# Two routers of a two-layer backbone get expert groups beside them, taken from the stages behind

## The reference

```python
def peer(h, wq, keys, u_tab, v_tab):
    q = (x @ wq).reshape(N, PEER_HEADS, 2, PEER_DKEY // 2)          # 8 heads
    s = jnp.einsum('nhpd,hpkd->nhpk', q, keys)                      # 2 x 128 scores
    top_s, top_i = lax.top_k(s, K)                                  # K = 16, twice
    cand = top_s[:, :, 0, :, None] + top_s[:, :, 1, None, :]
    best_s, best = lax.top_k(cand.reshape(N, PEER_HEADS, K * K), K)
    ...
    expert = (i1 * PEER_NKEYS + i2).reshape(N, PEER_HEADS * K)      # 128 experts a token
    gate = jax.nn.softmax(best_s, axis=-1)
    ...
        a = jax.nn.gelu(jnp.einsum('tkd,td->tk', u_tab[eb], xb), approximate=False)
        return jnp.einsum('tk,tkd->td', gb * a, v_tab[eb])
```

## Time and profile before

| what | us |
|---|---|
| median of 3 runs | 5934.2 |
| lowest and highest | 5932.68, 5950.15 |
| the profiled execution | 5949.2 |
| its span, first to last instruction | 5947.1 |
| PE busy in it | 4117.5 (69%) |
| DVE busy | 2900.9 (49%) |
| ACT busy | 1697.3 (29%) |
| POOL busy | 1441.5 (24%) |
| gathers, as a share of the 16 DMA engines | 56.4% |
| loads by SP, as such a share | 16.6% |
| mean granted TensorE clock | 0.814 |

### The profile page before, as it was taken

One profiled execution on the slowest core, in us unless ns is written; L12 is line 12 of the kernel. 1 busy time (PEld: TensorE's weight loads), 2 busy tenths in 40 slices (PEclk: granted clock), 3 DMA queues, 4 the chain that ended last, 5 costly groups with the idle time before them and its releaser, 6 DMA issues.

```text
span 5947.1 us, 63889 instructions
## 1 busy us (share of the span) xinstructions
PE 4117.5 (69%) x22248; PEld 2506.1 (42%) x22248; DVE 2900.9 (49%) x6835; ACT 1697.3 (29%) x4733; POOL 1441.5 (24%) x1295
## 2 busy tenths in 40 slices
PE   3889477889886685548476677778468785545555
PEld 1677454566563443224132235677335453211111
DVE  0321747544438544664445444322854445654444
ACT  0200137332432342233322222201152442222222
POOL 0000022212221232223343341000023332235443
PEclk7779789969997897778788888669778898767777
DMA  6434367748886798679999995024378997689998
GB/s 257 151 130 162 121 248 281 290 170 319 329 343 234 302 420 328 266 274 386 379 409 411 394 420 200 27 67 155 117 286 361 369 402 318 256 335 421 407 417 358
DMA packets 259315, 1712.65 MB, mean 288 GB/s; under 512 B 37712, under 2 KB 39344, under 8 KB 71600
## 3 DMA queue, kind: packets, MB, share of 16 engines
q0 software_dynamic: 184320, 1342.26, 56.4%
q1 hardware_dynamic: 74672, 366.31, 16.6%
HBM read 1690.43 MB, written 17.92 MB: 287 GB/s over the span
## 4 chain that ended last, share of the span: by engine, by line
PE 42%; DMA 24%; DVE 15%; ACT 6%; issue 4%; DVEq 4%; POOL 3%; ACTq 2%; SPq 1%; PEldq 0%; PEld 0%; POOLq 0%
PE psum L423 25%; DMA arena<-in_uv,arena 21%; PE psum L774 10%; DVE arena L2020 3%; POOL arena L1108 3%; DVE arena L1932 1%; DVE arena L1925 1%; DMA arena<-in_w_ada 1%; DVE arena L1926 1%; PE psum L383 1%; PE psum L604 1%; PE psum L605 1%; ACT arena L1444 1%; ACT arena L1441 1%; PE psum L639 1%
## 5 line engine op out<-in xcount | busy, mean ns | idle before, releaser
L1108 POOL DMA_INDIRECT arena<-in_uv,arena x1280 | 1437.6, 1123 | 4469.9 <-PE psum L774 3039.1
L774 PE MATMUL psum<-arena 64*64 64x512 f32 x10240 | 1564.5, 742 | 1086.5 <-ACTq L1445 990.9
L2020 DVE CUSTOM_DVE_ANT_0 arena<-arena 128x1024 f32<-128x1024 f32 x1280 | 1552.5, 1226 | 1330.0 <-DMA arena<-in_uv,arena 1272.4
L423 PE MATMUL psum<-arena 128*128 128x256 f32 (+2 forms) x8480 | 1945.9, 388 | 171.4 <-DVEq L1464 120.4
L423 PEld LDWEIGHTS psum<-arena 128*128 128x128 f32 (+1 forms) x8480 | 1616.9, 195 | 599.2 <-issue 194.1
L774 PEld LDWEIGHTS psum<-arena 64*64 64x64 f32 x10240 | 392.7, 157 | 2068.6 <-ACTq L1445 1375.8
L1438 ACT ACTIVATE arena<-arena 128x2 f32<-128x2 f32 x640 | 130.9, 205 | 1684.8 <-DVEq L2022 1671.3
L1444 ACT ACTIVATE arena<-arena 128x64 f32<-128x64 f32 x1280 | 376.2, 340 | 45.8 <-issue 1.8
L383 PE MATMUL psum<-arena 128*128 128x128 f32 (+1 forms) x680 | 129.4, 346 | 337.3 <-DVE arena L1523 119.8
L1441 ACT ACTIVATE arena<-arena 128x1 f32<-128x1 f32 x1280 | 307.6, 287 | 45.5 <-issue 1.3
L383 PEld LDWEIGHTS psum<-arena 128*128 128x128 f32 (+1 forms) x680 | 97.9, 178 | 391.2 <-issue 183.5
(11 more groups left out here) (210 smaller groups left out, 2747.4 us busy)
## 6 DMA issues: line engine op xcount, KB each, us to landing
arena<-in_w_in SPq DMA_DIRECT2D x92, 1024.0 KB, 5.9
arena<-in_w_mix SPq DMA_DIRECT2D x120, 768.0 KB, 7.3
arena<-in_w_ada SPq DMA_DIRECT2D x32, 1536.0 KB, 16.4
arena<-in_w_wq SPq DMA_DIRECT2D x40, 1152.0 KB, 6.0
arena<-in_w_wo SPq DMA_DIRECT2D x20, 1024.0 KB, 7.5
arena<-in_uv,arena POOLq DMA_INDIRECT x1280, 10.8
arena<-ada_rows SPq DMA_DIRECT2D x15, 512.0 KB, 5.6
arena<-x_rows SPq DMA_DIRECT2D x14, 512.0 KB, 6.2
```

Of the source, the lines that this page charges most:

```text
L423: ins = mm(out, a, b, start=(i == 0), stop=(i == last))
L774: ins = mm(psum[o, r_ * 512:r_ * 512 + 512], DIAG[rows, c, :], RING[rows, sl, D + half * 512:D + (half + 1) * 512], start=first, stop=last ...
L1108: pool.indirect_dma_start(RING[:, sl, :], None, io["uv"], bass.IndirectOffsetOnAxis(IDX[:, t, h * TOPK + k:h * TOPK + k + 1], 0)).then_inc ...
L2020: V_.tensor_tensor_reduce(out=RING[:, sl, 0:D], in0=RING[:, sl, 0:D], in1=XT[:, u % 2, :], scale=1.0, scalar=0.0, op0=ALU.mult, op1=ALU.ad ...
```

## The change

route(0,0) moves from the end of segment a to the start of b, and route(1,1) from the end of d to the start of e1, so that the groups of b and e1 are also spread over them. The order of the dense work stays as it was. The cost of a step of these two routers is 28 instead of 12, which only weighs how many groups they get. Since the groups beside these routers are of the tiles that the router is routing, `quotas` has a cap: behind step n of a router, no group of head n or later of its own pair may stand (`routed_upto`).

```diff
@@ steps
     if kind == "route":
-        return [12.0] * PH
+        return [(28.0 if (l, pairs) in FIRST_ROUTES else 12.0)] * PH
+FIRST_ROUTES = ((0, (0,)), (1, (1,)))
@@ schedule
-    a = [(k, 0, (0,)) for k in ("norm1", "qkv", "da", "mlp", "ml", "mc", "mln", "merge", "route")]
-    b = [(k, 0, both) for k in ("norm1", "qkv", "da", "mlp", "ml", "mc", "mln")] + [("merge", 0, (1,)), ("route", 0, (1,))]
+    a = [(k, 0, (0,)) for k in ("norm1", "qkv", "da", "mlp", "ml", "mc", "mln", "merge")]
+    b = [("route", 0, (0,))] + [(k, 0, both) for k in ("norm1", "qkv", "da", "mlp", "ml", "mc", "mln")] + [("merge", 0, (1,)), ("route", 0, (1,))]
-    d = [..., ("mln", 1, (1,)), ("merge", 1, (1,)), ("route", 1, (1,))]
-    e1 = [("q", 1, (2,)), ("da", 1, (2,)), ...]
+    d = [..., ("mln", 1, (1,)), ("merge", 1, (1,))]
+    e1 = [("route", 1, (1,)), ("q", 1, (2,)), ("da", 1, (2,)), ...]
+def routed_upto(items, l, pairs, heads):
+    for i, item in enumerate(items):
+        if item is not None:
+            (ul, t), g = UNITS[item[0]], item[1]
+            if (ul, (t // 2,)) == (l, pairs) and g * GS // TOPK >= heads:
+                return i
+    return len(items)
@@ quotas
-            for cost in steps(*st):
+            for n, cost in enumerate(steps(*st)):
                 cum += cost
                 want = lead + int(round((len(items) - lead) * cum / total))
+                if st[0] == "route" and n < PH - 1:
+                    want = max(done, min(want, routed_upto(items, st[1], st[2], n)))
```

More of the change, by code:

```diff
@@ L118, in schedule @@
     both = (1, 2)
-    a = [(k, 0, (0,)) for k in ("norm1", "qkv", "da", "mlp", "ml", "mc", "mln", "merge", "route")]
-    b = [(k, 0, both) for k in ("norm1", "qkv", "da", "mlp", "ml", "mc", "mln")] + [("merge", 0, (1,)), ("route", 0, (1,))]
+    a = [(k, 0, (0,)) for k in ("norm1", "qkv", "da", "mlp", "ml", "mc", "mln", "merge")]
+    b = [("route", 0, (0,))] + [(k, 0, both) for k in ("norm1", "qkv", "da", "mlp", "ml", "mc", "mln")] + [("merge", 0, (1,)), ("route", 0, (1,))]
     c1 = [("merge", 0, (2,)), ("route", 0, (2,))] + [(k, 1, (0,)) for k in ("norm1", "kv", "mlp", "ml")]
     c2 = [(k, 1, (1,)) for k in ("norm1", "qkv", "mlp", "mc")]
-    d = [("norm1", 1, (2,)), ("kv", 1, (2,)), ("mlp", 1, (2,)), ("edge", 1, (2,)), ("da", 1, (1,)), ("ml_back", 1, both), ("mln", 1, (1,)), ("merge", 1, (1,)), ("route", 1, (1,))]
-    e1 = [("q", 1, (2,)), ("da", 1, (2,)), ("ml_on", 1, both), ("mc", 1, (2,)), ("mln", 1, (2,)), ("merge", 1, (2,)), ("route", 1, (2,))]
+    d = [("norm1", 1, (2,)), ("kv", 1, (2,)), ("mlp", 1, (2,)), ("edge", 1, (2,)), ("da", 1, (1,)), ("ml_back", 1, both), ("mln", 1, (1,)), ("merge", 1, (1,))]
+    e1 = [("route", 1, (1,)), ("q", 1, (2,)), ("da", 1, (2,)), ("ml_on", 1, both), ("mc", 1, (2,)), ("mln", 1, (2,)), ("merge", 1, (2,)), ("route", 1, (2,))]
     p0 = sequence([0, 1])
```

## The result

| | us |
|---|---|
| before, median of 5 runs (the 3 of above and 2 more) | 5940.6 (5932.7 to 5950.2) |
| changed kernel, median of 5 runs | 5973.2 (5962.3 to 5992.1) |
| ratio, with its 95% interval | 1.0054 (1.004 to 1.0067) |
| forecast, range | 5959, 5910 to 6000 |
| the profiled execution of the changed kernel, its span | 5992.1, 5989.9 |

The kernel became slower by 32.6 us, 0.54%. The forecast was 24.8 us slower than the median it started from.

The account below looks back on a forecast made before the run. Lone routers were taken as VectorE chains with idle transfers, the first layer as bound by PE, the last stretch by transfers. 123 + 196 - 47 - 18 - 229 = +25 us on the median 5934.2 gave 5959, range 5910 to 6000.

Parts of the forecast that it names:

- Router (0,0), +123: Router (0,0), from 0 to 30 groups: 278.6 us against 155.7, so 123 us longer.
- Router (1,1), +196: Router (1,1), from 0 to 45 groups: 352.3 us against 156.1, so 196 us longer.
- the rival in which bursts are no dearer: Router (1,1) pays 4.07 us a group, as router (1,2) does, 183 us: +12, 5946 us, no change; chance 0.27.
- The value for each group past the fifth: In router bursts, each group past the fifth costs 5.2 us, the transfer rate.
- The rest of the first stretch, -47: Dense stages of segment b lose 26 groups at 1.88 us each and da(0,(1,2)) three: 47 us less.
- Router (0,1), -18: Router (0,1) has fewer groups; its first period falls from 32.9 to 22.6 us, three others by 2.6: 18 us less.
- The rest of the last stretch, -229: 45 groups leave merge(1,2), mc, da, ml_on, q and router (1,2): 229 us less, or 5.1 us a group.
- the two limits of 243 and 245: Merge(1,2) with 33 groups: PE's work takes 243 us, transfers at 402 GB/s take 245; forecast 249.
- What was charged nothing: Segments c1, c2, d and the tail keep their quotas, so no time was added for them.
- The last stretch gives more: All 45 groups leaving the last stretch give 6.1 us each, 275 in place of 229: 5913 us; chance 0.16.
- The slow rival, 243: Every group of router (1,1) pays 5.4 us, 243 in place of 196: +72, 6006 us; chance 0.13.

Follow-up runs that it names:

- the run with 8 groups: Only router (0,0) moved, its head cost 6 in place of 28, so 8 groups in place of 30, against the kernel before: 5942.1 us, ratio 0.9996.
- 17, 24 and 45 groups: Only router (1,1) moved, with head cost 8, 12 or 28, against the kernel before: ratios 0.9987, 1.0027 and 0.9947.

## Why the prediction was right, point by point

- **Router (0,0), +123.** +125.4. Its burst of seven took 50.0 us where I had 49.3, and the fours 34.6 to 35.0.
- **Router (1,1), +196.** +194.2, well above the 183 of the rival in which bursts are no dearer, and far from 243. The value for each group past the fifth, the transfer rate, is what the trace shows: 5.0 us a group. In the first burst of eight the fifth group ended 20.7 us behind the mark where I had 20.3, and three more at 5.0 us made 35.6 where I had 35.9. The periods of eight then came out 0.3 to 0.7 us shorter than said, that of seven 1.3 longer.
- **The rest of the first stretch, -47.** -39. Most dense stages gave what was said (mlp -14, ml -8, mc -10, merge(0,1) -11), but norm1 behind router (0,0) grew from 34.2 to 43.9 us. This is a cost that the record did not have: I followed SP's queue past XT and XP and charged nothing, but did not look at the loads behind the router. The token rows of norm1:

```profile
879.49 1.60 POOL L1121 DMA_INDIRECT arena<-in_uv,arena  x1 [0.31 <-issue]
...
880.45 1.25 SPq L901 DMA_DIRECT2D arena<-in_x  x2
893.08 1.06 ACT L1160 ACTIVATE arena<-arena 128x1024 f32<-128x1024 f32 x1 [16.11 <-DMA arena<-in_x]
```

  In the changed kernel they are issued behind gathers that POOL has just started (six in the 11 us before, of which the last is shown), and ScalarE has them 12.6 us later. In the kernel before nothing was under way, and it took 5.1 us:

```profile
751.98 0.80 SPq L888 DMA_DIRECT2D arena<-in_x  x2
...
757.06 1.06 ACT L1147 ACTIVATE arena<-arena 128x1024 f32<-128x1024 f32 x1 [10.29 <-DMA arena<-in_x]
```

  With one group a head (the run with 8 groups) POOL has issued nothing for 32 us when the load is issued; it takes 4.9 us again and norm1 36.4. So 7.5 of the 9.7 us are the late landing, and 2.2 stay without it. That the gathers delay the load is so supported from both sides; a run that issues the load earlier was not made.

  The shortfall of 8 us from the -47 can't be put to norm1 alone, though. In the run with the first move alone the same stages hold the same groups and norm1 is as long (43.4), and yet they fell by 48.8. The difference is ml(0,(1,2)); here it is in the kernel before (14 groups), in the changed kernel and in that run (11 each):

```profile
1191.10:1352.40 161.30, 136.20 (x728) 94.57 (x728) 82.35 (x202) 48.27 (x116) 30.00 (x26) 0.68 0.48 184
1310.90:1464.70 153.80, 133.41 (x680) 98.77 (x680) 72.81 (x188) 44.46 (x101) 23.82 (x23) 0.66 0.42 151
1309.70:1455.20 145.50, 124.84 (x680) 91.28 (x680) 72.83 (x188) 44.46 (x101) 25.32 (x23) 0.71 0.44 162
```

  The same work took 153.8 us at a granted clock of 0.66 and 145.5 at 0.71. So the -8 of ml is partly the clock of this execution, and I take the -39 as known to some 10 us.
- **Router (0,1), -18.** -16.0.
- **The rest of the last stretch, -229.** -228.6: merge(1,2) -93 (-91), mc -32 (-31), da -37 (-37), q and ml_on together -12 (-11), router (1,2) -55 (-59). Merge(1,2) took 246.6 us, close to the two limits of 243 and 245; I had 249 with no reason for the other 4; that PE's limit is near is shown by the run with half the bytes.
- **What was charged nothing.** Segments a (+3.0), c1, c2 and d up to merge(1,1) (+7.3) and the last groups (-3.5) together are 7 us longer in the trace of after. Their code and their groups are the same, and I put this to the two executions, which is not shown: by medians the whole change is 32.6 us and by spans 42.8. The record had 25, at the lower end of the 24 to 40 us that the interval of the ratio gives.
- **The rivals.** "The last stretch gives more" would have needed 275 us and got 229. The rule of the Trainium skill that spoke for it, to interleave regimes (Perfetto Trace Analysis, Optimization Strategy), holds for the second move by itself (ratio 0.9947) and fails for the first (1.012): in the first layer the regime that takes the groups out pays 1.9 us for each, and the router that takes them in 4. "Bursts no dearer" gave 5946, +12 us, which lies below all five runs and below the interval, and is 11 us short in router (1,1), where the waits refute it. The slow rival, 243, did not occur.

## What to carry to other kernels

Read the price of filling work as a curve over the size of the burst and not as a rate: here it is 2.6 us for each of the first two groups, 11 for the third, 1 for the fourth, and 4.8 on average for each from the fifth to the eighth (between 2.6 and 8), so that 17, 24 and 45 groups gain, lose and gain. The step in this curve was an order of instructions on one engine that could be changed; that was worth 1.5% by itself, more than the move that the profile's idle transfers suggested, and with bursts of four the two together gave 2.5%. Work taken from a stage pays what binds that stage, so price both ends before moving anything, and look which first load of the next stage now queues behind the transfers that were added.

## What the runs showed that I had not expected

- A full ring to which POOL adds nothing for a whole head (it waits 16.4 us) starts late: its first slot comes free 10.1 us behind the mark and the first row lands 6.8 us behind the issue. With half the bytes it lands 4.9 us behind it.
- Half the bytes are not half the transfer time. The last 128 groups, with 4 KB pieces in place of 8, took 484.5 us in place of 688.2, at a share of 0.84 and 293 GB/s in place of 0.98 and 399. By busy share that is 349 GB/s in place of 407, in one execution.
- The same stage with the same groups, ml(0,(1,2)), took 153.8, 145.5 and 140.2 us in three executions of three kernels, at granted clocks of 0.66, 0.71 and 0.74. A change of some microseconds in a stage that PE binds should be read beside the clock.
